# The low half of a weight chunk in four GpSimd instructions of 256 columns instead of one of 1024

## The reference, cut to what matters

```
h = modulate(rmsnorm(x, norm_ffn_g[i]), sh2, sc2)
gate, up = jnp.split(h @ w_ffn_in[i], 2, axis=-1)
x = x + g2[:, None, :] * ((jax.nn.silu(gate) * up) @ w_ffn_out[i])
mod = c_act @ w_ada[i] + b_ada[i]      # one vector for each of 14 groups: ada_raw, ada_acc
```

## Time and profile before

| | |
|---|---|
| runs, us | 1772.79, 1776.90, 1779.14; median 1776.9 |
| span of the profiled execution | 1779.9 us (no other time is given for it) |
| TensorE matmul busy | 1642.5 us, 92% |
| VectorE busy | 878.0 us, 49% |
| GpSimd busy | 641.3 us, 36% |
| ScalarE busy | 596.6 us, 34% |

### The profile page before, as it was taken

How to read it: one execution, slowest core, us unless ns; L and a number is a source line. 1 busy time by engine, 2 the same in 40 slices (tenths; PEclk the granted TensorE clock), 3 DMA queues, 4 the chain that set the end, 5 groups by cost and what they waited for, 6 DMA issues and landing times.

```text
span 1779.9 us, 20253 instructions
## 1 busy us (share of the span) xinstructions
PE 1642.5 (92%) x7156; PEld 1330.3 (75%) x7156; DVE 878.0 (49%) x1039; ACT 596.6 (34%) x843; POOL 641.3 (36%) x263
## 2 busy tenths in 40 slices
PE   6898898896798898899999999999998899999997
PEld 4677677675677686788877888888786688788875
DVE  6666656787776556413335453442615633113314
ACT  5343343444332222122324443434433422212223
POOL 3342242332433333344443333253341344344431
PEclk9998899998998898899999999999999999999999
DMA  5334234431534656523223222132221132222221
GB/s 191 140 120 153 106 118 164 155 131 36 195 113 142 212 200 224 178 95 99 101 84 104 95 70 95 59 105 82 81 101 41 57 109 94 95 95 95 94 83 48
DMA packets 56927, 202.83 MB, mean 114 GB/s; under 512 B 6320, under 2 KB 6320, under 8 KB 56880
## 3 DMA queue, kind: packets, MB, share of 16 engines
q1 hardware_dynamic: 55728, 198.73, 32.3%
q10 hardware_dynamic: 1152, 3.45, 0.6%
HBM read 200.05 MB, written 2.10 MB: 114 GB/s over the span
## 4 chain that ended last, share of the span: by engine, by line
PE 57%; issue 21%; DVE 8%; POOL 6%; DMA 5%; ACT 2%; SPq 0%; POOLq 0%; DVEq 0%; ACTq 0%
PE banks L1241 16%; PE banks L1245 15%; PE banks L1244 15%; POOL w_lo L302 6%; DMA ada_raw<-in_ADA 4%; DVE ada_acc L698 3%; PE banks L1575 2%; PE banks L1572 2%; PE banks L1576 2%; DMA w_raw<-in_W 2%; PE banks L1615 1%; PE banks L1614 1%; PE banks L1616 1%; DVE b_lo L1051 1%; DVE b_lo L1097 1%
## 5 line engine op out<-in xcount | busy, mean ns | idle before, releaser
L302 POOL TENSOR_TENSOR w_lo<-w_raw,w_hi 128x1024 fp32r<-128x1024 f32 x259 | 641.1, 2479 | 1107.6 <-ACT w_hi L326 1107.5
L1241 PE MATMUL banks<-a_hi,w_lo 128*128 128x512 f32 x1328 | 536.9, 404 | 10.7 <-POOL w_lo L302 2.6
L1244 PE MATMUL banks<-a_lo,w_hi 128*128 128x512 f32 x1328 | 528.6, 398 | 0.0
L1245 PE MATMUL banks<-a_hi,w_hi 128*128 128x512 f32 x1328 | 527.9, 398 | 0.0
L326 ACT ACTIVATE w_hi<-w_raw 128x1024 fp32r<-128x1024 f32 x259 | 273.3, 1058 | 740.7 <-PE banks L1241 579.8
L1241 PEld LDWEIGHTS banks<-a_hi,w_lo 128*128 128x128 f32 x1328 | 257.4, 194 | 68.5 <-issue 4.5
L1244 PEld LDWEIGHTS banks<-a_lo,w_hi 128*128 128x128 f32 x1328 | 257.4, 194 | 54.6 <-issue 1.7
L1245 PEld LDWEIGHTS banks<-a_hi,w_hi 128*128 128x128 f32 x1328 | 256.5, 193 | 55.2
L1241 PE MATMUL banks<-b_hi,w_lo 128*128 128x512 f32 x560 | 223.9, 400 | 23.1 <-DVE b_lo L1051 12.9
L1245 PE MATMUL banks<-b_hi,w_hi 128*128 128x512 f32 x560 | 221.1, 395 | 0.0
L1244 PE MATMUL banks<-b_lo,w_hi 128*128 128x512 f32 x560 | 221.0, 395 | 0.0
(11 more groups left out here) (194 smaller groups left out, 1532.3 us busy)
## 6 DMA issues: line engine op xcount, KB each, us to landing
w_raw<-in_W SPq DMA_DIRECT2D x259, 512.0 KB, 3.2
ada_raw<-in_ADA SPq DMA_DIRECT2D x112, 512.0 KB, 4.0
X<-in_XT SPq DMA_DIRECT2D x8, 256.0 KB, 6.0
out<-X SPq DMA_DIRECT2D x8, 256.0 KB, 2.2
scr<-in_DECAY ACTq DMA_DIRECT2D x4, 448.0 KB, 3.3
scr<-in_PT ACTq DMA_DIRECT2D x1, 512.0 KB, 4.9
scr<-in_ROPE ACTq DMA_DIRECT2D x1, 512.0 KB, 3.6
cols<-in_COLS ACTq DMA_DIRECT2D x1, 292.5 KB, 4.1
```

What stands on the lines that cost most here:

```text
L302: pool.tensor_tensor(w_lo[:, c % RING, :], w_raw[:, c % RING, :], w_hi[:, c % RING, :].bitcast(fp32), ALU.subtract).then_inc(wlo, 1)
L1241: mm = pe.matmul(out, lo, x_hi, start=first, stop=False)
L1244: pe.matmul(out, hi, x_lo, start=False, stop=False)
L1245: mm = pe.matmul(out, hi, x_hi, start=False, stop=last)
```

## The change

GpSimd's one instruction for a chunk becomes four, for columns 0 to 255, 256 to 511, 512 to 767 and 768 to 1023. Each adds 1 to `wlo`, which thus counts quarters. All who wait for `wlo` wait for four times the number they waited for before, so TensorE and SyncE still go on only when the whole chunk is done.

```diff
+QUARTERS = 4
+QW = 1024 // QUARTERS
...
+    def pieces(self, c):
+
+        return QUARTERS * c if self.i is None else self.i * (QUARTERS * self.per["chunk"]) + QUARTERS * c
...
-                    sp.wait_ge(wlo, at("chunk", c - RING + 1))
+                    sp.wait_ge(wlo, at.pieces(c - RING + 1))
...
                 pool.wait_ge(whi, at("chunk", c + 1))
-                pool.tensor_tensor(w_lo[:, c % RING, :], w_raw[:, c % RING, :],
-                                   w_hi[:, c % RING, :].bitcast(fp32), ALU.subtract).then_inc(wlo, 1)
+                for q in range(QUARTERS):
+                    part = slice(q * QW, (q + 1) * QW)
+                    pool.tensor_tensor(w_lo[:, c % RING, part], w_raw[:, c % RING, part],
+                                       w_hi[:, c % RING, part].bitcast(fp32), ALU.subtract).then_inc(wlo, 1)
...
-                    pe.wait_ge(wlo, at("chunk", c + 1))
+                    pe.wait_ge(wlo, at.pieces(c + 1))
```

More of the change, by code:

```diff
@@ L1473, in _ @@
                         if begins:
-                            pe.wait_ge(wlo, CH["dft1"] + 1)
+                            pe.wait_ge(wlo, flat.pieces(CH["dft1"] + 1))
                         xh, xl = (a[:, 2 * g + k, tt * P:(tt + 1) * P] for a in (a_hi, a_lo))
@@ L1495, in table @@
                     begun.add(c)
-                    pe.wait_ge(wlo, c + 1)
+                    pe.wait_ge(wlo, flat.pieces(c + 1))
                 w = slice((tt % 2) * S, (tt % 2) * S + NF)
```

## The result

Four runs each gave a median of 1729.0 us (1724.5 to 1741.1) with the change and 1778.0 us (1772.8 to 1780.3) without it: a ratio of 0.974, with a 95% interval of 0.970 to 0.978. The kernel is faster by 49 us.

What follows compares the result with a forecast made beforehand. TensorE, busy 92%, was taken as the bound, with only its 137 us of idle time to win. Gains of -35.1 and losses of +4.0 made -31 us, 1749 from the profiled span or 1746; the forecast said 1748, range 1732 to 1772.

Steps and rivals of the forecast that it cites:

- 1, "up" stage ends: Four "up" stage ends: lone line 1051 blocked 0.1 us in place of 1.6; -1.5 each, -6.0 us.
- 2, "up" loop with ada: Five turns of the "up" loop: line 1051 and two of line 698 blocked less, 1.8 us a turn; -9.0 us.
- 3, attention gap, four turns: Attention loop, gap 4.50 us before line 1359: lines 822 and 872 blocked less; -2.3 each, -9.2 us.
- 3, its wait for `ada_acc`: Attention loop, TensorE's wait for `ada_acc` 15 us after the gap, 0.7 us, goes in three turns; -2.2 us.
- 4, gate: Gate stage, gap 10.22 us: lines 967 and 969 wait less, -1.0 in two rounds; -2.0 us.
- 5, after the Fourier stage, and 545 us: Gap 4.77 us after the Fourier stage, four of line 995 shorter, -3.0; gap at 545 us, one line 698, -1.2.
- 6, the five smaller gaps named: Gaps at 27, 312, 351, 432 and 1389 us, one collision in each chain; -2.5 us together.
- all other gaps (forecast: norm stages): Norm stages where both engines are saturated pay the low half's extra 0.3 us; +1.0 us.
- 7, two waits for low halves: At 445 and 463 us TensorE's low half comes 0.3 + 1.2 us later, as VectorE gets in first; +3.0 us.
- rival C: TensorE's gaps stay for other reasons, loads and ScalarE, once VectorE is earlier: no change, 1773 us, chance 0.07.
- A: Rival: no hand-over to VectorE between quarters, so collisions on TensorE's chain last 0.3 us longer: slower, 1788 us, chance 0.11.
- B: Rival: a dear quarter, fixed part over 0.10 us, paid by about 70 collisions on the chain: 1755 to 1771, chance 0.12.

Runs made afterwards that it cites:

- the kernel without reading: Against the change: GpSimd subtracts only a chunk's first two columns and zeroes the rest by three memsets (low half left out of the result); 1677.3 us, one run.
- the fillers: Kernel before plus unread matmuls put in for TensorE's gaps: attention loop, four 1777.0 us, three 1775.0 us; "up" stage ends, two placements, 1787.0 and 1781.4 us.

## Why the prediction was wrong, by its own steps

**The step that failed** stands in the first paragraph: "only its idle time, 1779.9 - 1642.5 = 137 us, can be won by a change that leaves its matmuls as they are". The matmuls were left as they are and their busy time fell by 27.8 us. A sum of waits, which the whole part on the change is, prices a gap at its length, and the lower end of the range, 1732, was added up from idle time in the same way. Here a gap also has what the clock takes behind it: of the 49 us, 26 are clock. The row for it stood in the list: of two turns of the "up" loop, the one with a clock of 1.00 is busy 28.39 us with 134 matmuls, the one with the long gap has 0.83. I read the idle times in it and gave the clock beside them no term.

**The sum of waits held.** TensorE's idle time fell by 29.6 us where the sum said 31, and by 28.0 in the mean of two profiles of each kernel (137.5 and 136.5; 107.9 and 110.1). Its busy time fell by 20.7 in that mean (1642.5 and 1633.3; 1614.7 and 1619.7), and 28 + 21 = 49 is the difference of the medians. The profiles of one kernel differ by up to 10 us in busy time, so the 28 and the 21 are known to a few microseconds only. Counted by the clock over all runs the split is 26 to 23; by this account 5 us of the half clock that is gone had cost nothing, as TensorE was idle in it.

By terms, before and after, TensorE's idle time in each:

| term | forecast | measured | |
|---|---|---|---|
| 1, "up" stage ends | -6.0 | -8.7 | three gaps 2.31 to 0.71, that at 712 us 5.99 to 2.06 |
| 2, "up" loop with ada | -9.0 | -8.1 | 15.3 to 7.2 in five turns |
| 3, attention gap, four turns | -9.2 | -11.2 | 4.50 to 1.71 each |
| 3, its wait for `ada_acc` | -2.2 | +0.7 | 0.74, 0.79, 0.74 to 0.78, 1.48, 0.74 |
| 4, gate | -2.0 | -2.2 | 10.22 to 8.00 |
| 5, after the Fourier stage, and 545 us | -4.2 | -3.9 | 4.77 to 1.68, 4.64 to 3.80 |
| 6, the five smaller gaps named | -2.5 | -4.2 | that at 27 us gone, that at 312 1.2 longer |
| all other gaps (forecast: norm stages) | +1.0 | +5 | at 56.9 us 0.76 to 2.85, at 287.2 us 1.65 to 3.49 |
| 7, two waits for low halves | +3.0 | +2.8 | 1.93 to 3.34, 2.64 to 4.05 |

- *Items 1 and 2.* The three lone gaps gave -1.6 each, where -1.5 was forecast. The 3.9 us at 712 are mostly chance: in the second profile of the kernel before that gap is 2.73 us and not 5.99, and with quarters it is 2.06 and 2.28. In the mean of two profiles of each kernel that gap and the five of the loop give -8.9, where the forecast had -10.5.
- *Item 3*: the reordering of line 872 against the low half came as worked out. The second wait didn't go, since the last of line 698 in front of it waits for its load of `ada_raw`. That is the mistake that rival C described, at one place.
- *Item 6* came out for the gaps that it named, with more than was forecast. What has no term is that other gaps grew by 5 us together. Several stand behind a chain of VectorE instructions, each of which can meet a quarter of its own; that this is the cause I take from what the forecast said of chains, and no run tests it.
- *Item 7* is right. The timeline of its first place has GpSimd's four quarters at 4.50 us, since two of the ada line ran ahead of the first and between them, and TensorE behind them:

```profile
416.34 2.95 DVE L706 SCALAR_TENSOR_TENSOR ada_acc<-ada_raw,small,ada_acc 128x1024 f32<-128x1024 f32 x2
416.72 4.50 POOL L310 TENSOR_TENSOR w_lo<-w_raw,w_hi 128x256 fp32r<-128x256 f32 x4 [8.63 <-ACT w_hi L334]
...
421.28 0.28 PE L1512 MATMUL banks<-w_lo,b_hi 128*1 128x258 f32 x1 [3.34 <-POOL w_lo L310]
```

**The price of a quarter** was 0.70 us from start to start, where the forecast had 0.68. By the five sizes (1, 128, 256, 512 and 1024 columns) the records last 0.19, 0.46, 0.74, 1.30 and 2.40 us, that is 0.19 us and 2.17 ns a column; back to back the pieces begin 0.14, 0.42, 0.70 and 1.25 us apart, so a further piece costs 0.14. That lies between the forecast's 0.10 and its bound of 0.20.

**The rivals.** *A* is refuted for quarters: `b_lo` takes its own 693 ns, and with a long first piece the block and the old time are back. *B*: a fixed part of 0.14 in place of 0.10 should cost 3 us by its rule; the idle time fell short of the sum by 1.4 to 3. *C* holds at one wait only. That a VectorE instruction waits for the whole of GpSimd's holds beside a subtraction, to 0.14 us: in the rows of the timeline line 1051 begins its 0.69 us that much before the recorded end. Beside memsets that read nothing, in the kernel without reading, the line that makes `b_lo` takes at most 695 ns, and VectorE in all 677.4 us in place of 756.5.

**What stays open.** How much the clock alone would give in the other stages wasn't tried; the fillers show 7 to 8 us of loss regained in one stage, of which the medians keep 1 to 3, and some 3 us behind two gaps of one run in another. Why equal gaps are followed by half clock in one run and not in another, no trace here shows. How the 50 us of the kernel without reading split between VectorE's waits, an earlier low half and the zeros isn't settled either.

## What to carry to other kernels

Where two engines hold each other up for whole instructions, as GpSimd's subtraction and VectorE's `b_lo` did here (2335 ns in the median beside 2.40 us, 1229 beside 1.30, 693 beside 0.74), the length of the block follows that of the instruction: cut that of the engine with slack, down to where the fixed part (0.14 us for each further piece here) eats the slack, and choose the number for the stage in which that engine then works, which is some chunks ahead of the one that multiplies. Price every TensorE gap twice, once by its length and once by the clock behind it: span times (1 - mean clock) gives a bound for the whole loss in one line, for every run, and here it fell by 25.9 us, the rest by 23.0. Where a few microseconds decide, compare means over runs, not one profile with one: the loss to the clock alone was 67 to 84 us in the runs of the kernel before.

## What was unexpected of the hardware

- VectorE gets in between GpSimd instructions that stand back to back with no wait and no signal: 693 ns for `b_lo` in the median of 44 with quarters. It isn't without exception: with eight pieces, one line was passed over at four boundaries running, in three turns of eight.
- A memset on GpSimd, of 340 columns in 0.38 us, holds up none of VectorE's instructions with two SBUF inputs (`b_lo` 691 to 695 ns, `ada_acc` 1274 to 1287), but a one-input instruction of two columns took up to 671 ns beside it in place of 169.
- Around and behind gaps the granted clock is 0.50 for 3.4 to 13.7 us at a time in one profile of the kernel before, and the 2.3 us gap at the end of the last "up" stage is followed by it in one profile and not in another (0.53 and 1.00 in the 3.4 us behind it). The mean clocks of that kernel's runs give a loss of 67 to 84 us each.
